# Gate loads and first-branch loads issued by GpSimd behind its stores, no longer by SyncE

## The reference, cut to what matters

```python
proj = einsum('btd,dc->btc', rmsnorm(x), w_in)
xa, za, v, bg, cg, zb, ga, gb = split(proj)
ya = pool_mixer(xa) * silu(za)                 # first branch
yb = bg * conv_mixer(cg * v) * silu(zb)        # second branch
merged = (sigmoid(ga + b_a) * einsum('bte,ed->btd', ya, w_proj_pool)
          + sigmoid(gb + b_b) * einsum('bte,ed->btd', yb, w_proj_conv))
y = rmsnorm(x + einsum('btd,de->bte', merged, w_out))
```

## Time and profile before

| | us |
|---|---|
| median of 3 runs | 2509.36 (2508.5 to 2511.25) |
| the profiled execution, its time | 2511.8 |
| its span, first to last instruction | 2509.7 |
| TensorE busy | 2453.1 (98%) |
| VectorE busy | 1581.5 (63%) |
| ScalarE busy | 888.5 (35%) |
| GpSimd busy | 109.7 (4%) |
| VectorE's busy tenths, in slices of 62.7 us, 1757 to 2133 us | 6, 5, 6, 7, 7, 7 |

### The profile page before, as it was taken

One profiled execution on the slowest core, in us unless ns is written; L12 is line 12 of the kernel. 1 busy time (PEld: TensorE's weight loads), 2 busy tenths in 40 slices (PEclk: granted clock), 3 DMA queues, 4 the chain that ended last, 5 costly groups with the idle time before them and its releaser, 6 DMA issues.

```text
span 2509.7 us, 44784 instructions
## 1 busy us (share of the span) xinstructions
PE 2453.1 (98%) x18786; PEld 2446.5 (97%) x18786; DVE 1581.5 (63%) x2293; ACT 888.5 (35%) x1499; POOL 109.7 (4%) x214
## 2 busy tenths in 40 slices
PE   6999999999999999999999999999999999989997
PEld 6999999999999999999999999999999999989997
DVE  6554444444444486776877877756656777768765
ACT  6433333233323343333322222233424334444454
POOL 2000000000000000000000000000000010100000
PEclk9999999999999999999999999999999999999999
DMA  6354333333333354443343333445547767566796
GB/s 222 135 191 157 104 105 105 105 105 105 104 101 101 130 190 147 151 157 137 127 153 136 109 131 136 152 155 187 191 156 241 264 236 248 172 229 227 251 298 183
DMA packets 219351, 409.80 MB, mean 163 GB/s; under 512 B 9449, under 2 KB 172445, under 8 KB 202576
## 3 DMA queue, kind: packets, MB, share of 16 engines
q1 hardware_dynamic: 195552, 274.49, 33.0%
q0 software_dynamic: 22656, 126.68, 13.7%
q10 hardware_dynamic: 944, 5.77, 0.6%
HBM read 277.72 MB, written 129.18 MB: 162 GB/s over the span
## 4 chain that ended last, share of the span: by engine, by line
PE 90%; DMA 4%; DVE 3%; issue 2%; ACT 1%; SPq 0%; POOL 0%; DVEq 0%; ACTq 0%; POOLq 0%
PE ps L1019 85%; PE ps L1193 3%; DMA ops_raw<-opq 1%; PE ps L1116 1%; DMA raw<-in_w_in_dram 1%; DMA raw<-in_w_out_dram 1%; DVE lo L1487 1%; DVE sb L1506 0%; ACT hi L1214 0%; DMA opm_raw<-opq 0%; DVE opm L1542 0%; PE ps L1135 0%; DMA raw_b<-pb 0%; DVE pb L1536 0%; PE ps L1092 0%
## 5 line engine op out<-in xcount | busy, mean ns | idle before, releaser
L1019 PE MATMUL ps<-ops,hi 128*128 128x272 f32 x10784 | 1475.0, 289 | 11.8 <-DVE pb L1536 9.8
L1019 PEld LDWEIGHTS ps<-ops,hi 128*128 128x128 f32 x10784 | 1406.8, 189 | 13.1 <-DVE pb L1536 10.4
L1019 PE MATMUL ps<-ops,lo 128*128 128x272 f32 x5392 | 785.6, 288 | 0.0
L1019 PEld LDWEIGHTS ps<-ops,lo 128*128 128x128 f32 x5392 | 717.9, 188 | 0.0
L1536 DVE TENSOR_TENSOR pb<-pb,ps 128x544 f32<-128x544 f32 x426 | 306.6, 720 | 367.7 <-PE ps L1019 367.5
L1214 ACT ACTIVATE hi<-sb 128x512 fp32r<-128x512 f32 x440 | 278.5, 633 | 622.4 <-PE ps L1019 551.0
L1487 DVE TENSOR_TENSOR lo<-raw,hi 128x512 fp32r<-128x512 f32 x392 | 270.0, 689 | 275.0 <-ACT hi L1214 272.7
L1487 DVE TENSOR_TENSOR lo<-sb,hi 128x512 fp32r<-128x512 f32 x440 | 302.3, 687 | 205.8 <-ACT hi L1214 204.1
L1214 ACT ACTIVATE hi<-raw 128x512 fp32r<-128x512 f32 x392 | 247.4, 633 | 444.1 <-PE ps L1019 393.9
L1238 ACT COPY pb<-ps 128x544 f32<-128x544 f32 x216 | 132.7, 614 | 422.7 <-PE ps L1019 410.7
L1019 PE MATMUL ps<-opm,hi 128*128 128x384 f32 x896 | 176.7, 338 | 10.4 <-DVE pbm_early L1536 9.2
(11 more groups left out here) (145 smaller groups left out, 1049.3 us busy)
## 6 DMA issues: line engine op xcount, KB each, us to landing
raw<-in_w_in_dram SPq DMA_DIRECT2D x158, 512.0 KB, 4.0
pb<-part SPq DMA_DIRECT2D x39, 1088.0 KB, 6.2
part<-pb POOLq DMA_DIRECT2D x37, 1088.0 KB, 5.0
raw<-in_w_out_dram SPq DMA_DIRECT2D x63, 512.0 KB, 5.0
ops_raw<-opq SPq DMA_DIRECT2D x18, 1088.0 KB, 7.4
gates<-pb POOLq DMA_DIRECT2D x16, 1088.0 KB, 8.1
gate<-gates SPq DMA_DIRECT2D x32, 544.0 KB, 6.6
opq<-ts POOLq DMA_DIRECT2D x12, 1088.0 KB, 5.0
```

Source lines behind the costliest of these rows:

```text
L1019: mm = nc.tensor.matmul(ps[b][:, c, 0:n], w[:, w_slot, kt * P:(kt + 1) * P], operand[:, kt, half, k * n:(k + 1) * n], start=fresh and kt = ...
```

## The change

Both helpers and their calls move from SyncE's stream to GpSimd's. Their waits, their sources and their destinations stay the same, and so do their slots. On GpSimd they stand behind the slot's `store_pair` and `store_states`.

```diff
         @block.sync
-            def load_gate(k, c):
-                i = 2 * k + c
-                if i < 2:
-                    sp.wait_ge(pb_stored[2], stored_before_gates)
-                else:
-                    sp.wait_ge(gated, i - 1)
-                w = FIRST[H1] + ORDER.index(GA + k)
-                sp.wait_ge(pb_stored[ring(w)], stored_after[w])
-                sp.dma_start(gate[c][:, :], gates[k, :, c, :]).then_inc(gate_landed[c], 16)
-            def load_first_branch(j, c):
-                i = 2 * j + c
-                if i < 2:
-                    sp.wait_ge(states_stored, 64)
-                else:
-                    sp.wait_ge(merged, i - 1)
-                w = FIRST[YA] + j
-                sp.wait_ge(pb_stored[ring(w)], stored_after[w])
-                sp.dma_start(ma[c][:, :], part_a[j, :, c, :]).then_inc(ma_landed[c], 16)
...
-                i, c = j, q - 3 if j == 0 else q
-                if r is not None and r >= 2:
-                    i, c = NOUT - 1, {10: 0, 12: 1}.get(r, -1)
-                if ph in (YA, YB) and 0 <= c < 2:
-                    load_gate((ph - YA) * NOUT + i, c)
-                    if ph == YB:
-                        load_first_branch(i, c)
         @block.gpsimd
+            # load_gate and load_first_branch as above, with pool in place of sp
...
                 if q == 4 and ph == H1 and CONV0 < j <= GB0 and (j - CONV0) % 4 == 0:
                     store_pair(g - 1)
+                a = g - g % 2
+                r = s - NQ * a if in_couple(g) else None
+                i, c = j, q - 3 if j == 0 else q
+                if r is not None and r >= 2:
+                    i, c = NOUT - 1, {10: 0, 12: 1}.get(r, -1)
+                if ph in (YA, YB) and 0 <= c < 2:
+                    load_gate((ph - YA) * NOUT + i, c)
+                    if ph == YB:
+                        load_first_branch(i, c)
                 if s - 2 in SUMS_AT and ph == H0:
                     store_sums(SUMS_AT[s - 2])
```

More of the change, by code:

```diff
@@ L728, in load_blocks @@
                 sp.dma_start(tb_in[:, :, :], opq[H1][:, 0:4, kt, :]).then_inc(tb_landed, 16)
-            def load_gate(k, c):
-                i = 2 * k + c
-                if i < 2:
-                    sp.wait_ge(pb_stored[2], stored_before_gates)
-                else:
-                    sp.wait_ge(gated, i - 1)
-                w = FIRST[H1] + ORDER.index(GA + k)
-                sp.wait_ge(pb_stored[ring(w)], stored_after[w])
-                sp.dma_start(gate[c][:, :], gates[k, :, c, :]).then_inc(gate_landed[c], 16)
-            stored_before_gates = max(stored_after[g] for g in range(FIRST[YA]) if ring(g) == 2)
-            def load_first_branch(j, c):
-                i = 2 * j + c
-                if i < 2:
-                    sp.wait_ge(states_stored, 64)
-                else:
-                    sp.wait_ge(merged, i - 1)
-                w = FIRST[YA] + j
-                sp.wait_ge(pb_stored[ring(w)], stored_after[w])
-                sp.dma_start(ma[c][:, :], part_a[j, :, c, :]).then_inc(ma_landed[c], 16)
             def load_mix(i):
@@ L903, in _, with load_gate, load_first_branch @@
                 pool.dma_start(opq[H1][:, i, :, :], h1raw[:, 2 * kq, :, th * TH:(th + 1) * TH]).then_inc(h1_stored, 16)
+            def load_gate(k, c):
+                i = 2 * k + c
+                if i < 2:
+                    pool.wait_ge(pb_stored[2], stored_before_gates)
+                else:
+                    pool.wait_ge(gated, i - 1)
+                w = FIRST[H1] + ORDER.index(GA + k)
+                pool.wait_ge(pb_stored[ring(w)], stored_after[w])
+                pool.dma_start(gate[c][:, :], gates[k, :, c, :]).then_inc(gate_landed[c], 16)
+            stored_before_gates = max(stored_after[g] for g in range(FIRST[YA]) if ring(g) == 2)
+            def load_first_branch(j, c):
+                i = 2 * j + c
+                if i < 2:
+                    pool.wait_ge(states_stored, 64)
+                else:
+                    pool.wait_ge(merged, i - 1)
+                w = FIRST[YA] + j
+                pool.wait_ge(pb_stored[ring(w)], stored_after[w])
+                pool.dma_start(ma[c][:, :], part_a[j, :, c, :]).then_inc(ma_landed[c], 16)
             def store_sums(e):
```

## The result

The changed kernel takes 2515.44 us (median of 20 runs, 2511.01 to 2519.55). The kernel before, run 20 times beside it, takes 2510.09 us. The ratio is 1.0018, 95% interval 1.0012 to 1.0025. So the change costs 3 to 6 us: a loss small enough to lie inside the 0.2% that the prediction called no change, but a real one. The predicted time was 2510.6 us, and the measured one lies within the range of 2505.5 to 2516.5. The one of before (2511.8 us) stood 1.7 us above the 2510.09 of its 20 runs. So the two traces differ by 1.6 us in their spans, where the medians differ by 5.3.

A forecast was written before the change was run, and what follows sets the result against it. TensorE, busy 98%, was taken as the bound, stalling mainly when seventh operand loads land late at YA and YB. Terms +2.7 - 2 + 0.5 = +1.2 us on the profiled 2511.8 gave 2513.0, median 2510.6 us, range 2505.5 to 2516.5.

The forecast's parts named there:

- its own sign: Forecast wrong if the chain of waits shows YB's four loads, or YA's operand lands as before.
- The opening reading: Second half of the run: nearly all TensorE waiting is three waits for a VectorE drain, 9.8 us together.
- Start of YB: Start of YB: -1 us for an earlier operand issue, 0 for a moved gate load, -1 for escaping the store.
- the bound of -4.3: Start of YB: the lower bound, if the seventh operand lands before 1953.6.
- the rival in which the stall goes with its clock: Start of YB: stall of 4.56 us and its half clock go, -6.5 us; 2502.9 or 2505.6; chance 0.12.
- this operand load can go about 1 us earlier: Start of YB: the fifth operand's load no longer waits behind a gate load, everything queued behind gains too: -1 us.
- The step on YB's first loads: Start of YB: the first gate and first-branch loads, now behind the store, touch the operand neither before nor after.
- The rival's mechanism, lateness handed on: Inside YB: late `ma` delays sums, stores and next loads; near 2514 to 2540; chance 0.14 beyond 2514.4.
- The other mechanism: VectorE's two-port modes lock GpSimd out while it writes descriptors; no large effect expected, included in the 0.14 chance.
- the prediction's own term: End of YB: the loads stand behind the store ScalarE waits for; +0.5 us, bounds -0.5 to +3.
- the rival with the start of YA and no gain at YB: Start of YA alone: no gain at YB and a longer half clock, +5.2 us, near 2514.6; chance 0.16.
- Inside YA: Inside YA: gate loads come after their pair's store from the second pair on, still in time; cost 0.

The follow-up runs named there:

- run 20: Not a run's label, but part of "run 20 times": the kernel before, unchanged, timed 20 times beside the changed kernel: 2510.09 us.
- after_again: The changed kernel run once more for a second profiled execution, nothing altered: 2514.16 us.
- yb_only: The kernel before, but all gate and first-branch loads of YB go to GpSimd's queue, those of YA stay with SyncE: ratio 1.0014.
- yb_inner_only: The kernel before, but only the loads of YB's pairs 1 to 6 go to GpSimd's queue: ratio 1.0010.
- before_again: The kernel before run once more for a second profiled execution, nothing altered: 2508.79 us.
- inner_before_store: As yb_inner_only, but GpSimd issues the four loads ahead of the store of the pair before, not behind it: ratio 1.0008 to the kernel before.
- all_moved_mended: The changed kernel with last stores of H1 and YA held until the next phase's seventh operand lands, inner YB loads ahead of the store: 2504.3 us, ratio 0.9973.
- stores_held: The kernel before, but GpSimd issues the last stores of H1 and YA only once the next phase's seventh operand has landed: 2504.89 us, ratio 0.9975.
- after: The changed kernel, all gate and first-branch loads on GpSimd, in its first profiled execution: 2513.11 us there, median 2515.44 us, ratio 1.0018.

## Why the prediction was right, and where not

**In short.** The time fell into the range, and the start of YA came as worked out. The size did not: +1.2 us was forecast and +5.3 measured, with an interval of 3 to 6 us. By its own sign (wrong if the chain of waits shows the gate or first-branch loads) the part on YB failed: `ma<-part_a` is in the chain for 9.85 us. The opening reading also left out a second group of TensorE's waits in the second half of the run, 9.2 us for `pbm_early` in M0 and M1. The change doesn't touch them (9.1 us after).

**Start of YA: right.** The operand load was put at +2.7 us and measured +2.8 (10.10 to 12.87), TensorE's wait at 7.3 and measured 7.38, in three traces 7.31 to 7.54. The turns of the queues predict it: the gate loads, issued behind the store, overtake the operand, and from 1778.5 to 1780 us the trace has 105 packets of GpSimd's queue against 104 of SyncE's. The Trainium skill (DMA: Bandwidth & Descriptors, "Queues, rings and completion order") states these turns as a rule, and the trace agrees. The low clock was taken as 0 with bounds of 1 us, and the rows give 6.50 us at 0.56, a loss of 2.9 us against the 1.5 of before, so +1.4. The whole leg is +3.9. But after_again, behind a wait of 7.31 us, loses only 1.5, and yb_only, whose wait of 4.09 us is that of before, loses 2.9. So the +1.4 is seen in one execution and isn't shown to come from the change.

**Start of YB: the sum had the right sign, its steps are not borne out.** -2 us was predicted. The trace has -3.3 for the wait and about -2.2 for the low clock that no longer comes, together -5.5, between the bound of -4.3 and the rival in which the stall goes with its clock, -6.5. The step "this operand load can go about 1 us earlier" came true for the fifth operand (1939.7 us, in a trace that is 3.6 us later there, against 1937.12), but not for the seventh (1949.24 against 1945.57). It can't be the cause: yb_inner_only leaves all YA loads on SyncE and has 9.2 us. The step on YB's first loads fits: moved alone they changed nothing (1.0001). Part of the gain is also the first trace's high start, since before_again has 10.1 and 2.38, not 12.3 and 4.56. What is left isn't explained: in the six traces with late inner loads the operand lands after 8.7 to 9.4 us, in the others that keep the store after 10.1 to 12.3. inner_before_store has the same list on SyncE and the same work up to YB's second pair on GpSimd, and is slow. The cause stays open.

**Inside YB: the place was right, the price of being tight was not.** The landings were put 1.3 to 2.2 us before the merges and the cost at 0. The trace has VectorE waiting three times, 0.7, 0.4 and 0.4 us. The rival's mechanism, lateness handed on, is seen at the sixth pair. VectorE is 1.13 us late there (0.70 + 0.43), GpSimd's last store stands 2.2 us behind the start of ScalarE's idle time (2084.36 to 2086.55), which was 1.1 before (2085.89 to 2086.99), and it lands after 8.3 us, not 7.0. ScalarE's wait of 8.16 becomes 10.49, and TensorE stops for 0.88 and 1.82 instead of 0.60 us. The lateness does not grow from pair to pair into TensorE stops, so the 2540 us of that rival is far off, and its +3 at the end of YB is about what happened (the prediction's own term was +0.5, with bounds to +3).

The lead that was spent shows at the third pair: before, its first gate load was issued at 1994.34 and landed after about 7.1 us, 10 us before its merge (2011.15). After, it was issued at 2001.04, behind the stores, for a merge at 2009.63. The other mechanism that the prediction put into this rival, VectorE holding up GpSimd's descriptors, doesn't show: the 48 issues took 0.53 us each, as before.

**End of YB and the sum.** The end is about +4 us with its low clock, not +0.5, and +2.3 to +2.7 without it. The forecast of +1.2 us for the profiled execution came out at +1.3 in time (2511.8 to 2513.11), and that is luck. Two terms, the start of YA and the end of YB, were too small by 1.2 and 3.5 us. A start of YB that was 3.5 better and 0.9 us less before YA and behind M0's first product made up for them. In the medians that gain isn't there in full: +5.3 us, near the rival with the start of YA and no gain at YB, 2514.6. Timed runs give the inner YB loads a loss (1.0010 and 1.0014). Against the first trace of before their traces show a net of about zero or below. Against before_again (span 2506.7) yb_inner_only is +2.4, which is the size of its ratio, with +3.0 in the fourth leg, and yb_only -0.3. So the end of YB is the likely place of the timed cost, but single traces don't show it. Restoring their lead took the waits away in the trace but did not move the time measurably (1.0008 against 1.0010). First-pair loads and inner loads, 0.0015 and 0.0010 alone, sum to 0.0025 against 0.0018 together, which the intervals allow.

**Inside YA: right.** In the second pair GpSimd issued the loads at 1808.2 behind the states, and no VectorE wait on a gate appears there.

## What to carry to other kernels

Before a transfer is moved to another queue, ask which transfer on the old queue it used to stand behind: the order in one queue protected the critical load, and on the other queue the same bytes take turns with it. The same reasoning finds gains: a store that nobody waits for, held back until the critical load has landed, was worth 6 us here (two such stores together), more than any placing of the loads. The traces find 2.4 to 2.7 us of that at the start of YA and not all of the rest. A load issued behind a store inherits the store's waits, so count its lead in the order of that queue, and where the lead falls from 10 us to 1, expect the odd wait to surface at the next place without slack.

## What the runs showed of the hardware

The low clock after a wait of TensorE doesn't follow the length of the wait. Its loss (busy time times one minus the granted share) was as follows in the 14 traces:

| wait of TensorE, us | loss behind it, us |
|---|---|
| 0.38 to 1.69 | none, in all such waits of the table above and of the stops for ScalarE |
| 1.75 to 1.84 | 1.7 six times, none three times |
| 2.38 to 3.32 | 1.6 to 3.0, and none in all_moved_mended after 3.32 |
| 3.82 to 4.62 | 1.5 to 2.9 |
| 7.31 to 7.54 | 1.5, 2.9, 2.9 |

TensorE in all_moved_mended around its wait of 1.75 us, and in stores_held around the same wait:

```profile
1784.00:1790.00 6.00, 4.77 (x39) 1.00 0.50 204
```

```profile
1784.00:1790.00 6.00, 4.63 (x24) 0.72 0.11 39
```

The same kernel has both: a wait of 1.82 us in after was followed by the low clock, and one of 1.83 at the same place in after_again by none. So making a stall shorter gives back its length, and sometimes 1.5 to 3 us of clock on top.

One kernel's executions spread over 8.5 us here (2511.0 to 2519.6), more than the whole effect. Single traces were still exact about the start of YA (12.8, 12.9 and 13.0 us in the three with the gate loads in front) and misleading about the sum: yb_only's profiled execution, 2508.20 us, was the fastest of its 11 runs, 5 us below their median.
